# One core, two transformer blocks with gathered experts: the expert sums in the four quarters of the array, eighty candidate pairs instead of 256, and plain fp32 projections with weights five tiles ahead

## What is computed

```python
s1 = jnp.einsum('bshd,nd->bshn', q[..., 0, :], sub_keys1).astype(jnp.float32)
s2 = jnp.einsum('bshd,nd->bshn', q[..., 1, :], sub_keys2).astype(jnp.float32)
v1, i1 = lax.top_k(s1, TOPK_HALF)          # 16 of 128
v2, i2 = lax.top_k(s2, TOPK_HALF)          # 16 of 128
cand = (v1[..., :, None] + v2[..., None, :]).reshape(B, S, PEER_HEADS, TOPK_HALF * TOPK_HALF)
cand_idx = (i1[..., :, None] * N_KEYS + i2[..., None, :]).reshape(B, S, PEER_HEADS, TOPK_HALF * TOPK_HALF)
top_v, pos = lax.top_k(cand, TOPK)         # 16 of 256
expert_idx = jnp.take_along_axis(cand_idx, pos, axis=-1)
gates = jax.nn.softmax(top_v, axis=-1).astype(h.dtype)
...
u = jnp.take(expert_down, idx_blk, axis=0)
act = jax.nn.gelu(jnp.einsum('bpd,bphkd->bphk', h_blk, u))
vv = jnp.take(expert_up, idx_blk, axis=0)
return jnp.einsum('bphk,bphkd->bpd', g_blk * act, vv)
```

## Time and profile before

| | us |
|---|---|
| median of 3 runs | 4798.39 |
| lowest, highest | 4793.35, 4800.57 |
| the profiled execution, its time | 4805.03 |
| the profiled execution, its span | 4803.1 |
| PE busy, share of the span | 3588.4 (75%) |
| DVE busy, share of the span | 2793.6 (58%) |
| bytes read from memory | 1241.76 MB, 259 GB/s over the span |

### The profile page before, as it was taken

How to read it: one execution, slowest core, us unless ns; L and a number is a source line. 1 busy time by engine, 2 the same in 40 slices (tenths; PEclk the granted TensorE clock), 3 DMA queues, 4 the chain that set the end, 5 groups by cost and what they waited for, 6 DMA issues and landing times. The chain is left out here.

```text
span 4803.1 us, 41734 instructions
## 1 busy us (share of the span) xinstructions
PE 3588.4 (75%) x13654; PEld 2096.5 (44%) x13654; DVE 2793.6 (58%) x6402; ACT 1104.7 (23%) x2607; POOL 1146.8 (24%) x1028
## 2 busy tenths in 40 slices
PE   4947587884676787877797775796868876677777
PEld 3834586562242332633375542452346653222222
DVE  5557765348653877544564567653655557755554
ACT  1104001121221212324432221222533121111111
POOL 0000000002432444222222232231222223333332
PEclk9978787997898998988899897897989988999999
DMA  4500000125896999878688787685668877899998
GB/s 177 181 32 3 4 1 20 57 72 236 342 374 273 404 412 374 323 256 311 222 333 297 268 316 274 262 314 204 246 244 328 310 286 306 346 377 420 416 420 360
DMA packets 202356, 1248.85 MB, mean 260 GB/s; under 512 B 24796, under 2 KB 29276, under 8 KB 67428
## 3 DMA queue, kind: packets, MB, share of 16 engines
q0 software_dynamic: 147456, 1073.81, 57.0%
q1 hardware_dynamic: 54184, 172.51, 10.6%
q10 hardware_dynamic: 512, 0.03, 0.0%
HBM read 1241.76 MB, written 4.46 MB: 259 GB/s over the span
## 5 line engine op out<-in xcount | busy, mean ns | idle before, releaser
L215 POOL DMA_INDIRECT held_pair<-in_experts,held_expert x1024 | 1146.6, 1120 | 3626.0 <-PE held_acc L233 2466.5
L277 DVE CUSTOM_DVE_ANT_0 held_pair<-held_pair,held_hrow 128x1024 f32<-128x1024 f32 x1024 | 1245.8, 1221 | 553.3 <-DMA held_pair<-in_experts,held_expert 507.9
L232 PE MATMUL held_acc<-held_pair,held_diag 128*128 128x512 f32 x2048 | 1150.9, 645 | 389.7 <-ACT held_diag L257 329.2
L233 PE MATMUL held_acc<-held_pair,held_diag 128*128 128x512 f32 x2048 | 1088.9, 614 | 0.0
L232 PEld LDWEIGHTS held_acc<-held_pair,held_diag 128*128 128x128 f32 x2048 | 352.9, 198 | 899.2 <-ACT held_diag L257 672.8
L257 ACT ACTIVATE held_diag<-held_ident,held_weight 128x128 f32<-128x128 f32 x1024 | 402.3, 393 | 1271.9 <-DVE held_weight L272 1254.1
L233 PEld LDWEIGHTS held_acc<-held_pair,held_diag 128*128 128x128 f32 x2048 | 405.3, 198 | 523.4 <-issue 523.4
L250 ACT ACTIVATE held_bent<-held_dot 128x2 f32<-128x2 f32 x512 | 102.9, 201 | 543.4 <-DVE held_dot L277 504.7
L500 PE MATMUL pgh_ps<-pgh_hhi,pgh_whi 128*128 128x256 f32 x384 | 127.6, 332 | 28.7 <-DVE pgh_wlo L519 28.7
L500 PE MATMUL p2h_ps<-p2h_hhi,p2h_whi 128*128 128x256 f32 x368 | 123.5, 336 | 31.7 <-DVE p2h_wlo L519 31.7
L1303 PE MATMUL c_ps<-c_keys,held_room 128*128 128x128 f32 x256 | 46.7, 366 | 131.7 <-DMA c_iota<-in_iota 131.7
(11 more groups left out here) (516 smaller groups left out, 5366.1 us busy)
## 6 DMA issues: line engine op xcount, KB each, us to landing
pgh_raw<-in_w_in SPq DMA_DIRECT2D x48, 512.0 KB, 7.2
p2h_raw<-in_w_in SPq DMA_DIRECT2D x46, 512.0 KB, 7.5
p_raw<-in_w_in SPq DMA_DIRECT2D x34, 512.0 KB, 3.4
p_w_ada<-in_w_ada SPq DMA_DIRECT2D x16, 1024.0 KB, 5.9
held_pair<-in_experts,held_expert POOLq DMA_INDIRECT x1024, 9.2
e2qh_raw<-in_w_peer_q SPq DMA_DIRECT2D x32, 512.0 KB, 7.3
ada_w<-in_w_ada SPq DMA_DIRECT2D x4, 2048.0 KB, 11.1
e1q_raw<-in_w_query SPq DMA_DIRECT2D x16, 512.0 KB, 3.6
```

The source lines that it names most:

```text
L215: pool.indirect_dma_start(self.pair[m % BUFS][:], None, self.layers[t // TT][0], bass.IndirectOffsetOnAxis(ap=self.expert[:, t % TT, s:s + ...
L232: pe.matmul(self.acc[0][:], diag[:], up[:, 0:512], start=s == 0, stop=s == NJ - 1)
L233: pe.matmul(self.acc[1][:], diag[:], up[:, 512:D], start=s == 0, stop=s == NJ - 1).then_inc(self.added, 1)
L277: ins = dve.tensor_tensor_reduce(down, down, self.hrow[:, t % TT, :], 1.0, 0.0, ALU.mult, ALU.add, self.dot[:, t % 2, s:s + 1])
```

## The change

Three edits, made together.

**The sums in four quarters.** `diag` becomes 128 x 64: rows 0 to 63 hold the diagonal matrix of tokens 0 to 63, and rows 64 to 127 that of tokens 64 to 127 (ACT scales a constant `bands`, two identities of 64 one above the other). In place of two products of 128 rows x 128 columns, a slot makes four of 64 x 64, each with 512 moving columns. The first two use rows 0 to 63 with columns 0 to 63 and rows 64 to 127 with columns 64 to 127, for half 0 of the up row; the other two use the two quarters that are left, for half 1. The sums land in the same two banks in another arrangement, and the addition to `xT` is cut in two pieces accordingly.

**Eighty pairs.** Of 256 pairs of two sorted lists only some can be among the 16 best. The change adds 80: the first list's best with all 16 of the second, entries 1 to 7 of the first with 0 to 7 of the second, and entries 8 to 15 of the first with the second's best. The five instructions then run over 80 values instead of 256, and six small instructions on 128 x 128 values are new, which turn a position 0 to 79 into the two list positions.

**Projections beside the gather.** `project_beside_stage` takes the place of `project_stage` in `mp`, `p2`, `pg`, `po` and `q`: plain fp32 products, 8 for a weight tile, no splits on ACT and DVE, and five weight tiles in flight. The three projections with 512 tokens (`p1`, `po1`, `e1q`) stay as they were.

```diff
+SPLIT = 2
+BAND, WIDE = P // SPLIT, D // SPLIT
...
-        self.diag = [r.sb(f"diag{u}", [P, P]) for u in range(DIAGS)]
+        self.diag = [r.sb(f"diag{u}", [P, BAND]) for u in range(DIAGS)]
...
+    def sum_of(self, i):
+
+        return self.acc[i * WIDE // 512][:, i * WIDE % 512:i * WIDE % 512 + WIDE]
...
             up, diag = self.pair[m % BUFS][:, D:2 * D], self.diag[m % DIAGS]
-            pe.matmul(self.acc[0][:], diag[:], up[:, 0:512], start=s == 0, stop=s == NJ - 1)
-            pe.matmul(self.acc[1][:], diag[:], up[:, 512:D], start=s == 0, stop=s == NJ - 1).then_inc(self.added, 1)
+            for turn in range(SPLIT):
+                for i in range(SPLIT):
+                    band, to = slice(i * BAND, (i + 1) * BAND), (i + turn) % SPLIT
+                    last = pe.matmul(self.sum_of(i)[to * BAND:(to + 1) * BAND], diag[band, :], up[band, turn * WIDE:(turn + 1) * WIDE],
+                                     start=s == 0, stop=s == NJ - 1)
+            last.then_inc(self.added, 1)
...
-            act.activation(self.diag[m % DIAGS][:], self.k.ident[:], ACT.Copy, scale=self.weight[:, t % 2, s:s + 1]).then_inc(self.diag_made, 1)
+            act.activation(self.diag[m % DIAGS][:], self.k.bands[:], ACT.Copy, scale=self.weight[:, t % 2, s:s + 1]).then_inc(self.diag_made, 1)
...
+                got, each = self.pt[:].rearrange("p (c n) -> p c n", n=P), WIDE // P
+                for i in range(u * SPLIT // 2, (u + 1) * SPLIT // 2):
+                    for to in range(SPLIT):
+                        chunk, first = (to - i) % SPLIT * each, i * each % 4
+                        x = self.xT[:, chunk:chunk + each, at + i * BAND:at + (i + 1) * BAND]
+                        new = got[:, first:first + each, to * BAND:(to + 1) * BAND]
+                        if gain is None:
+                            ins = dve.tensor_tensor(x, new, x, ALU.add)
+                        else:
+                            for c in range(each):
+                                ins = dve.scalar_tensor_tensor(x[:, c], new[:, c], gain[:, chunk + c:chunk + c + 1], x[:, c], ALU.mult, ALU.add)
+                ins.then_inc(self.moved, 1)
...
+def project_beside_stage(nc, name, w_dram, act_in, kc, chunks, dst, tokens, beats, add=None):
+
+    beats = beats.over(chunks)
+    with ExitStack() as stack:
+        r = Room(nc, stack, name)
+        w = [r.sb(f"w{u}", [P, kc, P]) for u in range(WEIGHT_TILES)]
+        ps = [r.ps(f"ps{u}") for u in range(4)]
+        made, used = r.sem("made", "used")
+        w_ready = [r.sem(f"w_ready{u}") for u in range(WEIGHT_TILES)]
+        with nc.Block() as block:
+            @block.gpsimd
+            def _(pool):
+                beats.pool(pool)
+
+            @block.sync
+            def _(sp):
+                for n in range(chunks):
+                    if n >= WEIGHT_TILES:
+                        sp.wait_ge(made, n - WEIGHT_TILES + 1)
+                    sp.dma_start(w[n % WEIGHT_TILES][:], w_dram[n]).then_inc(w_ready[n % WEIGHT_TILES], 16)
+
+            @block.scalar
+            def _(act):
+                for n in range(chunks):
+                    beats.act(act, n)
+
+            @block.tensor
+            def _(pe):
+                for n in range(chunks):
+                    pe.wait_ge(w_ready[n % WEIGHT_TILES], 16 * (n // WEIGHT_TILES) + 16)
+                    if n >= 4:
+                        pe.wait_ge(used, n - 3)
+                    for c in range(kc):
+                        last = pe.matmul(ps[n % 4][:, 0:tokens], w[n % WEIGHT_TILES][:, c, :], act_in[:, c, :], start=c == 0, stop=c == kc - 1)
+                    last.then_inc(made, 1)
+                    beats.pe(pe, n)
+
+            @block.vector
+            def _(dve):
+                for n in range(chunks):
+                    beats.dve(dve, n)
+                    dve.wait_ge(made, n + 1)
+                    got = ps[n % 4][:, 0:tokens]
+                    if add is None:
+                        ins = dve.tensor_copy(dst[:, n, :], got)
+                    else:
+                        gain, base = add
+                        ins = dve.scalar_tensor_tensor(dst[:, n, :], got, gain[:, n:n + 1], base[:, n, :], ALU.mult, ALU.add)
+                    ins.then_inc(used, 1)
+
+
+WEIGHT_TILES = 5
...
-        cand, cleft = r.sb("cand", [P, PH, 256]), r.sb("cleft", [P, PH, 256])
+        cand, cleft = r.sb("cand", [P, PH, PAIRS]), r.sb("cleft", [P, PH, PAIRS])
...
-                        link(dve.tensor_tensor(cand[:].rearrange("p h (a b) -> p h a b", b=K16),
-                                               bcast(v4[:, :, 0, :], K16, 3), bcast(v4[:, :, 1, :], K16, 2), ALU.add))
+                        one, two = v4[:, :, 0, :], v4[:, :, 1, :]
+                        dve.tensor_tensor(cand[:, :, 0:MID], one[:, :, 0:1].to_broadcast([P, PH, K16]), two, ALU.add)
+                        dve.tensor_tensor(cand[:, :, LAST:PAIRS], one[:, :, 8:K16], two[:, :, 0:1].to_broadcast([P, PH, 8]), ALU.add)
+                        link(dve.tensor_tensor(cand[:, :, MID:LAST].rearrange("p h (a b) -> p h a b", b=8),
+                                               bcast(one[:, :, 1:8], 8, 3), bcast(two[:, :, 0:8], 7, 2), ALU.add))
...
-                        posf = pos[:].rearrange("p h n -> p (h n)")
-                        link(dve.tensor_single_scalar(part[:, 0], posf, 4, ALU.logical_shift_right))
-                        link(dve.tensor_single_scalar(part[:, 1], posf, 15, ALU.bitwise_and))
+                        posu = pos[:].rearrange("p h n -> p (h n)")
+                        dve.tensor_copy(posf[:], posu)
+                        dve.tensor_single_scalar(part[:, 0], posu, 3, ALU.logical_shift_right)
+                        link(dve.tensor_single_scalar(part[:, 1], posu, 7, ALU.bitwise_and))
                         link(dve.tensor_copy(partf[:], part[:]))
+                        link(dve.tensor_scalar(flag[:], partf[:, 0], 1.0, 8.0, ALU.is_equal, ALU.mult))
+                        link(dve.tensor_tensor(partf[:, 1], partf[:, 1], flag[:], ALU.add))
+                        link(dve.scalar_tensor_tensor(partf[:, 1], posf[:], float(LAST), partf[:, 1], ALU.is_lt, ALU.mult))
+                        link(dve.tensor_scalar(partf[:, 0], partf[:, 0], 1.0, 0.0, ALU.subtract, ALU.max))
+                        link(dve.scalar_tensor_tensor(partf[:, 0], posf[:], float(LAST - 8), partf[:, 0], ALU.subtract, ALU.max))
...
-        project_stage(nc, "mp", k, ins["w_mem_kv"], mT, DC, DC, mkv, tokens=NMEM, beats=beats["mp"])
+        project_beside_stage(nc, "mp", ins["w_mem_kv"], mT, DC, DC, mkv, NMEM, beats["mp"])
...
-    project_stage(nc, own("p2"), k, ins["w_in_2"], h, DC, Y_GATE, z, tokens=HALF, beats=beats["p2"])
+    project_beside_stage(nc, own("p2"), ins["w_in_2"], h, DC, Y_GATE, z, HALF, beats["p2"])
...
-    project_stage(nc, own("po2"), k, ins["w_out_2"], h, DC, DC, x, tokens=HALF, add=(k.ones, x), beats=beats["po"])
+    project_beside_stage(nc, own("po2"), ins["w_out_2"], h, DC, DC, x, HALF, beats["po"], add=(k.ones, x))
...
+    a["bands"] = (q[:, None] % BAND == np.arange(BAND)[None, :]).astype(np.float32)
```

18 lines of the change are left out of this document (7 added, 11 removed).

## The result

The changed kernel took 4646.1 us (median of 4 runs, 4644.1 to 4648.0), beside 4795.9 for the kernel before on the same chip. The ratio is 0.9689, with a 95% interval of 0.9672 to 0.9706: 3.1% faster. The forecast was 4581 (4.5% faster), with a range of 4480 to 4715.

The account below looks back on a forecast made before the run. PE was taken to bound projections and merges, DMA the drain and `c23`, DVE the other choosers, with mixed limits from `hn` to `mema`. Terms -47 - 13 - 19 - 63 - 16 - 55 - 2.5 = -216 gave 4581 us, range 4480 to 4715.

Parts of the forecast that it names:

- A slot on PE at 0.88 us: All slots: four quarter products run at once on PE, so a slot costs 0.88 us instead of 1.72.
- the rivals of two or one at a time: PE slots: only two quarters at once, 1.74 us a slot, 4889 (12%); one at a time, 3.44, about 5900 (3%).
- The switches, at 0.35: PE: changing the array's division in and out costs 0.35 us per group of slots whose neighbours are full products.
- Projections: Eight PE-bound stages (`p2`, `pg`, `po`, `q`, twice): dearer tiles and switches, cheaper slots, earlier starts; together -47 us.
- Merges: The two merges, bound by PE: 38 slots give -32 us, 38 switches +13, together -19.
- `mp`: Memory projection stage: gets shorter until its 54.6 MB meet the DMA's pace, 146 to 133 us, -13.
- `c1` and `c23` together: Choosers with DMA about full: shorter PE and DVE work helps only at the ends, taken as -20 us.
- Norms and small memory stages: 39 slots in these stages: at most -33 us from cheaper slots, taken as -16.
- From `hn` to `mema`: Twice 75 slots, no new switches: at most -126 us of PE work, half taken as on the path, -63.
- a sign of being wrong: Prediction wrong if a slot exceeds 1.3 us, the `hn` to `mema` clock is below 0.8, or the drain's pace changes.
- clock rival: `hn` to `mema` clock falls to 0.70, adding 43 us a half, about 110 with norms and choosers: 4690 us; 12%.
- hidden behind DMA: `mp`, `c1`, `c23` gain nothing and nine starts each lose half of 6.4 us to weight loads: 4643 us; 13%.

## Why the prediction was right, and where its sizes were off

**What bounds the kernel** was read rightly for the projections, the merges, `mp`, `c23` and the drain: halving the bytes and changing the projection alone show it each time.

**A slot on PE at 0.88 us** held: four quarters at once, 0.86 us for the second slot of a pair, and the rivals of two or one at a time are out. The switches, at 0.35, are in the pitch of a tile with one slot: 3.46 + 0.88 + 0.35 = 4.69 forecast, 4.67 from 2387.09 to 2391.76. Less of it than forecast lies ahead of the host's next product (1.02 us, not 1.1 to 1.3), more behind it.

**Projections**, -47: -52 measured, and its two parts by themselves too: +74 for the new form (67 measured, in the kernel with that part alone), and -121 for slots and switches on top of it (968 us in that kernel, 849 with all three: -119). In the old form the slots give only 57, by the waits above because it lacks its weights in time. The five tiles ahead had been priced at the start alone, and there they gave less than that: 0.9 us in `pg` in place of 2.4, since the first weight now landed 5.2 us after its issue, not 3.7; 14.2 us of idle PE stayed.

**Merges**, -19: -18. **`c0`**, -6.9: -6.9. **Drain**: -2.5 forecast, -3 measured, and its pace held at a clock of 0.66.

**`mp`**, -13: -3. The step that failed: all 54.6 MB were divided by the drain's 410 GB/s, as if the DMA were full from the first to the last microsecond. The pace was right where it is full (409 GB/s over 117 us). But the first 13 us carried 251 GB/s and the last 13, when PE was done, 266: together these 26 us lost 10. `c23` is the same error: 412 GB/s over 330 us, but 113 and 328 in the 18 us at its ends, 17 us lost. `c1` and `c23` together gave 10 us, not 20. The four choosers of the second layer gave 22, not 28; half the bytes take another 15 and 26 us off the two pairs, so they are not bound by DVE alone, as the forecast had it. **Norms and small memory stages**, -16: -6. With half the bytes they lose 2 to 9 us each, so the gathers are on their path too; the forecast had weighed that for `mp`, `c1` and `c23` alone.

**From `hn` to `mema`**, -63: -31. This is the largest error, half of what the whole sum lacks. PE's work fell as counted: busy time by clock is 240 x 0.87 = 209 before and 204 x 0.73 = 149 after, -60 (63 forecast). But 149 at the clock of before would be 171 us of busy PE, and it was 204: the clock added 33 us in this half, and in the other 173 at 0.85 would be 204, where 234 were busy. At the half that the forecast put on the path, these 63 us are 32, the size of the gap. That part is arithmetic, and the half itself may be too large: PE's busy time fell by 37 and 40 us and the length by 14 and 18, a share of 0.4, by which the clock would make about 25 of the 32 us and the smaller share the rest. No run separates the two. Shown are the pieces, that the same `hn` takes 50 or 62 us and the same `foxa` 77 or 100 as the clock goes, and that giving PE its work back brings clock and length back together.

The prediction named as a sign of being wrong that this clock is below 0.8. It is 0.73, so by its own sign it had this stretch wrong, though the whole time lies in its range (and near the top of the forecast's own, 4490 to 4660). Its clock rival (12%) came true in the mechanism (0.70 forecast) and, in this stretch, at about a third of its 86 us, for it had put all of PE's added time on the path where the forecast had put half. In the choosers a clock of 0.65 to 0.76 cost little, for DVE was busy for 84.5 of 92 us.

**The whole**: -216 forecast, -150 by the medians. The sign, the slot's price and the projections were right. Missing are 32 us from `hn` to `mema`, 20 in `mp`, `c1` and `c23`, 10 in the norms and small stages and 6 in the last choosers, and the projections gave 5 more than forecast. 4646 is 3 us from the rival "hidden behind DMA" (4643, 13%), and that is chance: of its 33 us in `mp`, `c1` and `c23` 20 came, but the start of `pg` got 0.9 us shorter where it had each start get longer (3.2 us lost, 2.4 gained), and it has nothing from `hn` to `mema`, where the gap is largest.

## What to carry to other kernels

When a change takes work off PE in a stage where PE is only partly busy, price the clock with it: read the granted clock in stretches of 10 us, and count the lower level as likely. Divide a stage's bytes by the full pace only where the DMA is full, and price the stage's start and end by themselves: cut the window there and read the share. And a faster engine moves the limit to whatever is fetched just in time: the old projection, with two tiles ahead, got 57 us from the short slots where the new one, with five, got 119.
